# ScalarE's small steps of a small expert placed one weight split sooner

## The reference

```python
def swiglu(h, wg, wu, wd):
    return (jax.nn.silu(h @ wg) * (h @ wu)) @ wd

def moe_swiglu(h, w_router, w_gate, w_up, w_down):
    logits = (h @ w_router).astype(jnp.float32)
    top_v, top_i = lax.top_k(logits, TOP_K)
    top_w = jax.nn.softmax(top_v, axis=-1)
    gates = jnp.sum(jax.nn.one_hot(top_i, N_EXPERTS, dtype=jnp.float32) * top_w[..., None], axis=-2)
    ...
    for e in range(N_EXPERTS):
        y = y + gates[..., e:e + 1] * swiglu(h, w_gate[e], w_up[e], w_down[e])
    return y
```

## Time and profile before

| | us |
|---|---|
| median of three runs | 1429.4 |
| lowest, highest | 1425.54, 1433.12 |
| the profiled execution | 1420.63 |
| its span on the core | 1418.8 |

### The profile page before, as it was taken

One profiled execution on the slowest core, in us unless ns is written; L12 is line 12 of the kernel. 1 busy time (PEld: TensorE's weight loads), 2 busy tenths in 40 slices (PEclk: granted clock), 3 DMA queues, 4 the chain that ended last, 5 costly groups with the idle time before them and its releaser, 6 DMA issues.

```text
span 1418.8 us, 16608 instructions
## 1 busy us (share of the span) xinstructions
PE 1369.0 (96%) x6550; PEld 1143.2 (81%) x6550; DVE 1097.6 (77%) x871; ACT 940.6 (66%) x767; POOL 49.3 (3%) x51
## 2 busy tenths in 40 slices
PE   8999999999999999999999999999999999999887
PEld 7886788887988788877888878878887878888766
DVE  4786644556465988888898898798898889888796
ACT  3565534335455677777777788687777777777764
POOL 0000000000010000000000000000000000002000
PEclk9999999999999999999999999999999999999998
DMA  9744455555632899999999999999999989999993
GB/s 311 214 159 149 155 205 178 178 179 177 224 119 92 334 373 382 379 387 399 322 407 390 364 400 407 393 366 398 379 374 414 408 324 397 394 368 392 412 360 115
DMA packets 136643, 439.13 MB, mean 310 GB/s; under 512 B 11520, under 2 KB 28912, under 8 KB 120816
## 3 DMA queue, kind: packets, MB, share of 16 engines
q1 hardware_dynamic: 130688, 424.24, 80.0%
q0 software_dynamic: 3392, 12.07, 2.5%
q10 hardware_dynamic: 2480, 1.69, 0.4%
HBM read 432.20 MB, written 5.78 MB: 309 GB/s over the span
## 4 chain that ended last, share of the span: by engine, by line
PE 73%; DVE 17%; ACT 5%; DMA 3%; issue 3%; ACTq 0%; SPq 0%; DVEq 0%
PE ps L2003 18%; PE ps L2005 18%; PE ps L2004 18%; DVE lo L1286 12%; PE ps L2575 7%; PE ps L2495 4%; PE ps L2496 4%; ACT hi L790 2%; DMA raw<-in_od_w_gate_dram 2%; PE ps L2560 1%; DMA wr<-in_od_w_router_dram 1%; ACT work L1098 1%; DVE work L1312 0%; PE ps L2299 0%; DMA x<-in_x_dram 0%
## 5 line engine op out<-in xcount | busy, mean ns | idle before, releaser
L1286 DVE TENSOR_TENSOR lo<-raw,hi 128x2048 fp32r<-128x2048 f32 (+1 forms) x403 | 904.9, 2285 | 102.9 <-ACT hi L790 101.2
L790 ACT ACTIVATE hi<-raw 128x2048 fp32r<-128x2048 f32 (+1 forms) x403 | 766.8, 1914 | 206.4 <-PE ps L2005 157.0
L2003 PE MATMUL ps<-hi,xT_hi 128*128 128x512 f32 (+1 forms) x752 | 294.6, 392 | 7.2 <-DVE lo L1286 4.6
L2005 PE MATMUL ps<-hi,xT_lo 128*128 128x512 f32 (+1 forms) x752 | 290.0, 386 | 0.0
L2004 PE MATMUL ps<-lo,xT_hi 128*128 128x512 f32 (+1 forms) x752 | 289.7, 385 | 0.0
L2495 PE MATMUL ps<-hi,xT_hi 128*128 128x512 f32 x448 | 187.4, 418 | 12.0 <-DVE lo L1286 11.0
L2496 PE MATMUL ps<-lo,xT_hi 128*128 128x512 f32 x448 | 181.4, 405 | 0.0
L2003 PEld LDWEIGHTS ps<-hi,xT_hi 128*128 128x128 f32 x752 | 141.7, 188 | 38.3 <-issue 5.5
L2005 PEld LDWEIGHTS ps<-hi,xT_lo 128*128 128x128 f32 x752 | 141.4, 188 | 28.7
L2004 PEld LDWEIGHTS ps<-lo,xT_hi 128*128 128x128 f32 x752 | 141.6, 188 | 26.4
L2495 PEld LDWEIGHTS ps<-hi,xT_hi 128*128 128x128 f32 x448 | 88.5, 198 | 45.5 <-DVE lo L1286 19.9
(11 more groups left out here) (327 smaller groups left out, 1223.9 us busy)
## 6 DMA issues: line engine op xcount, KB each, us to landing
raw<-in_od_w_gate_dram SPq DMA_DIRECT2D x112, 1024.0 KB, 8.4
raw<-in_od_w_up_dram SPq DMA_DIRECT2D x112, 1024.0 KB, 9.4
raw<-in_od_w_down_dram SPq DMA_DIRECT2D x112, 1024.0 KB, 8.3
raw<-in_od_w_qkv_dram SPq DMA_DIRECT2D x12, 1024.0 KB, 5.2
raw<-in_ev_w_gate_dram SPq DMA_DIRECT2D x11, 1024.0 KB, 5.2
raw<-in_ev_w_up_dram SPq DMA_DIRECT2D x11, 1024.0 KB, 5.1
raw<-in_ev_w_down_dram SPq DMA_DIRECT2D x11, 1024.0 KB, 5.1
raw<-in_ev_w_in_dram SPq DMA_DIRECT2D x4, 1024.0 KB, 11.1
```

The lines of the kernel that those rows point to most:

```text
L790: act.activation(unit(hi, n), unit(raw, n), ACT.Copy).then_inc(hi_ready, 1)
L1286: dve.tensor_tensor(unit(lo, n), unit(raw, n), unit(hi, n).bitcast(F32), ALU.subtract)\
L2003: pe.matmul(out, s_hi, m_hi, start=start, stop=False, skip_group_check=True)
L2005: return pe.matmul(out, s_lo, m_hi, start=False, stop=stop, skip_group_check=True)
```

## The change

In the small experts' part of ScalarE's program the numbers given to `used` are one lower at every small step but the last few of the expert, so that each step stands behind one split fewer. Nothing else is edited; the other engines' instructions and all transfers are the same, and so is the order of ScalarE's small steps among themselves.

```diff
                     if e in SMALL:
-                        used(UP_AT[0])
+                        used(UP_AT[0] - 1)
                         keep_gate(e, 0)
-                        used(GATE_AT[1])
+                        used(GATE_AT[1] - 1)
                         keep_up(e, 0)
+                        used(GATE_AT[1] + 1)
+                        turned_silu(e, 0)
                         used(GATE_AT[1] + 2)
-                        turned_silu(e, 0)
-                        used(GATE_AT[1] + 3)
                         turned_high(e, 0)
-                        used(UP_AT[1])
+                        used(UP_AT[1] - 1)
                         keep_gate(e, 1)
-                        used(DOWN_AT[0])
+                        used(DOWN_AT[0] - 1)
                         keep_up(e, 1)
                         used(GATE_AT[2])
...
+                        used(GATE_AT[2] + 1)
+                        turned_silu(e, 1)
                         used(GATE_AT[2] + 2)
-                        turned_silu(e, 1)
-                        used(GATE_AT[2] + 3)
                         turned_high(e, 1)
-                        used(UP_AT[2])
+                        used(UP_AT[2] - 1)
                         turned_silu(e, 2)
                         keep_gate(e, 2)
-                        used(UP_AT[2] + 1)
+                        used(UP_AT[2])
                         turned_high(e, 2)
-                        used(DOWN_AT[1])
+                        used(DOWN_AT[1] - 1)
                         keep_up(e, 2)
...
+                        used(DOWN_AT[2] - 1)
+                        keep_up(e, 3)
                         used(DOWN_AT[2])
-                        keep_up(e, 3)
+                        turned_silu(e, 5)
                         used(DOWN_AT[2] + 1)
-                        turned_silu(e, 5)
+                        turned_high(e, 5)
                         used(DOWN_AT[2] + 2)
-                        turned_high(e, 5)
-                        used(DOWN_AT[2] + 3)
                         turned_silu(e, 6)
                         used(DOWN_AT[3])
```

More of the change, by code:

```diff
@@ L1165, in _ @@
                             act.activation(placeT[:], ps[:, 6, 0:SEQ], ACT.Copy).then_inc(placeT_ready, 1)
+                        used(GATE_AT[2] + 1)
+                        turned_silu(e, 1)
                         used(GATE_AT[2] + 2)
-                        turned_silu(e, 1)
-                        used(GATE_AT[2] + 3)
                         turned_high(e, 1)
-                        used(UP_AT[2])
+                        used(UP_AT[2] - 1)
                         turned_silu(e, 2)
                         keep_gate(e, 2)
-                        used(UP_AT[2] + 1)
+                        used(UP_AT[2])
                         turned_high(e, 2)
-                        used(DOWN_AT[1])
+                        used(DOWN_AT[1] - 1)
                         keep_up(e, 2)
+                        used(GATE_AT[3] + 1)
+                        turned_silu(e, 3)
                         used(GATE_AT[3] + 2)
-                        turned_silu(e, 3)
-                        used(GATE_AT[3] + 3)
                         turned_high(e, 3)
-                        used(UP_AT[3])
+                        used(UP_AT[3] - 1)
                         turned_silu(e, 4)
                         keep_gate(e, 3)
-                        used(UP_AT[3] + 1)
+                        used(UP_AT[3])
                         turned_high(e, 4)
+                        used(DOWN_AT[2] - 1)
+                        keep_up(e, 3)
                         used(DOWN_AT[2])
-                        keep_up(e, 3)
+                        turned_silu(e, 5)
                         used(DOWN_AT[2] + 1)
-                        turned_silu(e, 5)
+                        turned_high(e, 5)
                         used(DOWN_AT[2] + 2)
-                        turned_high(e, 5)
-                        used(DOWN_AT[2] + 3)
                         turned_silu(e, 6)
```

## The result

| | before | changed |
|---|---|---|
| median, us | 1428.37 (4 runs, 1425.54 to 1433.12) | 1460.46 (4 runs, 1454.05 to 1464.32) |
| profiled execution's span, us | 1418.8 | 1452.3 |

The ratio is 1.0226, with a 95% interval of 1.0192 to 1.0259: 32 us slower, where 30 were forecast. The profiled executions differ by 33.5.

What follows compares the result with a forecast made beforehand. VectorE's work after each turn was taken to bound small experts. Expert terms 8.2, 8.6, 8.6 and 4.9 sum to 30.3 us, taking the median from 1429.4 to 1459 us, range 1438 to 1475.

Steps and rivals of the forecast that it cites:

- What bounds a small expert: Small experts: time is set by what VectorE does in the microseconds after each turn, mainly its low parts.
- First, third, fifth and seventh turn: Expert 3: the split starts after SiLU, so VectorE's low part comes late by 1.5, 2.0, 1.9 and 1.45 us.
- Second, fourth, sixth turn: Expert 3: VectorE loses 1.5 us but gives it back waiting for the next turn; nothing, up to 1.5 each without idle.
- Start of the expert: Expert 3: the first gate copy waits for TensorE's use of two gate units, making the next high part late; 0.8 us.
- The up copies: After first and third turn: copy waits for TensorE's fourth up unit, delaying the next split; 0.5 us each, bounds 0 to 2.
- The walk: ScalarE's steps followed after expert 3's first turn: ScalarE is later than the landings, so the loss counts in full.
- Transfers as cover: Landings absorb nothing in experts 3 and 5 (other end 5.8 us an expert), but the first terms in expert 7.
- That rival, no change at all: Small experts are bound by transfers, which hide the loss: 1429 us at full cover; chance 0.07.
- The price of the clock: Small experts: expert 5 at clock 0.95 against expert 3 at 0.98, so 0.03 of granted clock costs 2.9 us.
- The signs that were named: Seven new VectorE waits, about 10 us in expert 3; 28 SiLU waits; fewer landing waits; small experts 8 us longer, large unchanged.
- The clock as a rival: Small experts: TensorE's granted clock drops a further 0.04, 16 us on top, 1475 us; chance 0.15.
- The rival on the fast side: Sixth turn waits for the fourth up copy; sooner copies free banks, up to 7 us faster, 1422 us; chance 0.03.

Runs made afterwards that it cites:

- SiLU alone: Against the kernel before, only ScalarE's SiLU and high parts, with gate copies of chunks 2 and 3, one split sooner: 1444.51 us, ratio 1.0100.
- the two runs with part of the turns: Against the kernel before, SiLU and high part one split sooner at turns 2, 4, 6 only: 1428.77 us, 1.0000; at 1, 3, 5, 7 only: 1445.06 us, 1.0103.
- the copies alone: Against the kernel before, only the up copies and first two gate copies one split sooner, SiLU and high parts unmoved: 1442.46 us, ratio 1.0079.
- halved transfers: Small experts' weight transfers move half the bytes: kernel before 1423.22 us, ratio 0.9950; changed kernel 1458.16 us, ratio 1.0184 against the kernel before.

## Why the prediction was right, and where its terms were off

*What bounds a small expert.* Right: VectorE's low parts after a turn. The most direct evidence is the pair of runs that move SiLU later: alone on ScalarE nothing, with VectorE's order too 17 us faster. No run moved VectorE's steps alone, so how much of the 17 us needs ScalarE's part of that edit stays open.

*First, third, fifth and seventh turn* (1.5, 2.0, 1.9, 1.45 us). The trace with SiLU alone shows 1.5, 1.9, 1.9 and 1.4 in position 3; the two runs with part of the turns show that these four carry it all (1.0103 against 1.0100).

*Second, fourth, sixth turn* (nothing). Right, and shown: 1.0000.

*Start of the expert* (0.8). Measured 1.0: TensorE's unit 4 starts 1.0 us late in all four small experts.

*The up copies* (0.5 after the first turn and 0.5 after the third). This is the term that was mis-sized. After the first turn the copy waits 1.32 us, and TensorE loses 1.7 us in position 3 between units 9 and 14; only 0.7 of this comes at unit 14, behind the up copy. After the third turn 0.5 to 0.8 is about right. Moved alone, the up copies cost 7.4 us in four experts, 1.9 each, or 6.0 us and 1.5 each when brought to equal clock, where the sum has 1.0. It was within the bounds named, 0 to 2 us each. I had taken VectorE's backlog for cover, but ScalarE, back to back, had no lead left to pass on.

*The second gate copy*. It has no term in the sum. The walk takes the copy behind the second split after the first turn as one that doesn't wait. In the changed kernel it waits 0.77 us, the low part of unit 10 waits 0.88, and TensorE loses 1.0 us at unit 10, the other part of the 1.7. In the four small experts the copy waits 0.78, 0.77, 0.89 and 0.98 us. With the copies alone the wait is 1.23 in all four, since there one split fewer stands between SiLU and the copy. In the changed kernel it came through TensorE's clock: the two gate units between the first turn and this copy take 5.1 to 5.3 us in all four small experts, part of it at half clock, where they take 3.74 at full clock. TensorE from the end of the first turn to the copy, position 3 (columns: us, PE busy, granted clock, DMA share, GB/s), changed kernel and then the copies alone:

```profile
847.34:852.41 5.07, 5.07 (x18) 0.74 1.03 426
```

```profile
842.82:846.56 3.74, 3.74 (x17) 1.00 1.03 424
```

The 1.3 to 1.6 us that the lower clock adds are more than the copy's wait, so at full clock the copy would not have waited. That is an estimate from these rows; no run of the changed kernel shows the place at full clock.

*Transfers as cover.* The walk said that landings cover nothing in positions 3 and 5 and the first terms in position 7. In position 3 the delay falls from 4.2 us at unit 14 to 3.8 at unit 18, so they cover 0.4. In position 7 it falls from 3.0 to 0.4 us behind the one long stretch that remains in the chain:

```profile
1338.69 11.13 DMA raw<-in_od_w_gate_dram
```

With halved transfers the cover is gone there (7.4 for 5.4 us). That rival, no change at all, is refuted by the same two runs.

*By experts.* Forecast 8.2, 8.6, 8.6, 4.9; measured 8.8, 9.9, 7.4, 5.4. The sum, 30.3 against 31.5, is closer than its parts, and that is in part luck: the second gate copy and the rest of the up copies came on top of it, while the clock of the changed kernel's runs was higher than that of the kernel before and took some back (33.0 us at equal clock, worked out below). Position 5 had three stretches at half clock before and has one now, which may be what takes back some of its loss.

*The stretches that were read.* The stretches of the earlier trace rows do not end with the experts. From first matmul to first matmul position 3 took 112.9 us before, not 107.70, and the large expert behind it 119.2, not 124.40. The rival of the transfers counted 42 landings of 2.55 us as 107.1 us, "just expert 3's 107.70"; against the true length they leave 5.8 us, so that support for it was an accident of the window. The sum does not use these lengths. The price of the clock does, 2.9 us for 0.03; by the true lengths it is 2.6 us (115.5 less 112.9) for 0.02 (0.98 to 0.96).

*The signs that were named.* The waits after turns came as forecast, seven of them, 11.5 us in all (about 10 named) and 1.38 to 2.30 us each. The five others, behind copies, were not among the signs. SiLU's waits stayed 28, ScalarE's waits for landings went, and the large experts kept their length.

*The clock as a rival* (0.04 less in small experts, 16 us more). Wrong in its sign on the whole, though a stretch at half clock has a part at one place, the second gate copy above. The granted clock of the small experts went from 0.96, 0.98, 0.96, 0.96 to 0.96, 0.99, 0.99, 0.97. The clock accounts for part of what the runs of the parts left open. Over the 65 single runs of the kernel before that stood beside these experiments, time and granted clock go together (four of the clocks, with 30 of the runs):

| granted clock | runs | mean us |
|---|---|---|
| 0.978 | 7 | 1432.8 |
| 0.980 | 8 | 1431.3 |
| 0.983 | 10 | 1428.1 |
| 0.986 | 5 | 1425.0 |

A line through all 65 falls by 9.4 us for each 0.01 (correlation -0.86). Their mean clock is 0.9814; that of the six runs with SiLU moved alone is 0.9878, of the six with the copies moved 0.9837, of the four of the changed kernel 0.9848. Brought by that line to the clock of before, the mean of SiLU's move costs 20.8 us instead of 14.7, the copies' 14.6 instead of 12.4, the whole change 33.0 instead of 29.8. By this line, then, half and more of the gap between the 25 us that I expected of SiLU's move and its plain 14 goes with the clock. By TensorE's first matmuls the four experts lose 5.0, 7.3, 3.7 and 4.8 us in its trace, together 20.8 as well, but this agreement is weak support: the two traces have unlike clocks (0.986 before, 0.990 with SiLU moved), and the profiled execution of the kernel before (1420.63 us) is faster than any of the 65. The 4 us that are left lie in positions 1 and 5, where the old trace has half-clock stretches; that these hid waits is my reading. The correction is worked out from runs of one kernel and carried over to others; no run sets the clock by itself.

The rival on the fast side (a turn waits for its up copy) had no row for it in any trace here.

## What to carry to other kernels

Where one engine's in-order program holds both a stream and small steps that wait for a third engine, ask for each small step what the stream's consumer wants first after the wait, and keep that item ahead of the step; more lead than that brought nothing here (0.9996), one item less cost 1.4 to 2.0 us, about the 1.9 of a split, at each wait that sets the end. Before moving a copy ahead, compare the time at which it is reached with the time at which its data are there: ahead of that time it is a wait, and everything behind it is late. If the consumer idles at such a wait, try moving its own step back together with the producer's, as the run that gained 17 us did. When the losses of several moved steps are told apart in a trace, follow the delay unit by unit: here 1.7 us between units 9 and 14 came from two copies, 1.0 and 0.7.

## What the runs showed of the hardware

A DMA share of 1.00 isn't a bound by itself: with half the bytes in small experts the share of position 3 fell from 1.00 to 0.67, and its length did not fall (112.9 us and 115.4, the second at a granted clock of 0.96 for 0.98). Position 7 went from 0.87 to 0.55, and the kernel's time fell by 8 of 1431 us.

TensorE's granted clock changes between executions of the same program (0.975 to 0.988 in 65 runs), and most of the spread of its times goes with it: 1435.6 us at 0.975 (2 runs), 1423.0 at 0.988 (1 run). From the first expert on, and without the end of the program, the stretches at half clock (1.2 GHz instead of 2.4) stand almost all in small experts, ten of them in the trace of the kernel before. More idle time on TensorE between units did not go with more of them: the kernel with SiLU moved has 7, the changed one 8, the faster one with both engines later 8, the one with up copies moved 15, each counted in one trace. One place repeats. The two gate units behind the first turn run in part at half clock in all four small experts of the changed kernel (granted clock 0.69 to 0.74), in two of four before, and in none of four with the copies alone (1.00). What decides this stays open.
